# A decoder layer with dilated attention, short convolution and 32 experts: experts packed four to three blocks, and other orders around them

## The chip, the core and the metric

The kernel runs on one core of a Trainium2 chip. Its engines are TensorE (PE in the profile), VectorE (DVE), ScalarE (ACT), GpSimd (POOL) and SyncE (SP), which only issues transfers here. Each engine works through its own instructions in order and waits on semaphores; 16 DMA engines move data. The metric is the device time of one execution in microseconds, the median of several runs.

## The reference, cut to what matters

1024 prompt tokens and 32 sample tokens (8 sequences of 4) go through one layer. All is float32. The part around the change is this:

```python
h = h + mixed                                  # attention and convolution, one output projection
m = rms_norm(h, g_ffn)
g_sel = top_k(softmax(m @ w_router_group), 1)  # one of 4 groups
top_v, top_i = top_k((m @ w_router_expert)[group g_sel], 2)   # two of its 8 experts
hidden = silu(m @ w_gate[e]) * (m @ w_up[e]) * gates          # per chosen expert, 256 wide
h = h + sum over both experts of hidden @ w_down[e]
gate = sigmoid(rms_norm(h, g_ple) @ w_ple_gate)
h = h + (p @ w_ple_proj) * gate                # p: an embedding of 256 per token
```

Each of the 1056 tokens has two of 32 experts, so 2112 rows are worked on, 66 per expert in the mean. The router depends on the data.

## The kernel before

The order of work is written out by hand: each engine has its own program, and semaphores join them. Tokens come in nine tiles: eight prompt tiles of 128 rows, then one of 32 (the sample). There are seven parts: the input projection, the convolution, the attention over the prompt (32 steps, a pair of heads and a tile each, listed in `STEPS`), the attention of the sample over its cache, the output projection with the routing, the experts, and the last stage with the embeddings.

**Output projection and routing.** For tile t TensorE runs `out_att(t)`, `router(t-1)` (transposes of the normalised tile), `rank(t-2)`, `out_conv(t)`, `logits(t-1)`. VectorE adds the residual in two parts, `make_m` multiplies by the reciprocal root and the gain, `choose` finds the experts, and `place` works out where the token stands in its expert's list. `make_m` needs the sum of squares (ScalarE) and the root. GpSimd stores the tile m in DRAM (`store_m`) and writes the token numbers to the lists in DRAM (`enlist`), and after the last tile the lists of the first four experts are loaded. VectorE then orders the other 28 experts by their number of rows, largest first.

**Experts.** A block is 128 rows. `PLAN` says how the 28 ordered experts fall into blocks: F is one expert with up to 128 rows, P a pair with up to 64 rows each, in two column strips of TensorE's array. With the four first experts this makes 27 blocks; experts with more rows than their place holds get overflow blocks, which run only if there are any. Weights (3 MB an expert) go through four slots. A planner in Python gives each load its slot and the block after which the slot is free: SP loads gate and up weights when the up products of that block are done, and the down weights when its down products are done, in the order of the loads. In block n TensorE runs `up(n)`, `down(n-1)`, `trans_rows(n+1)` (transposes of the gathered rows, copied by VectorE in `take_rows`), `trans_hidden(n)`. GpSimd's program for the blocks is

```python
        for n in range(NBM):
            if n + NSTAT + 1 < NBM:
                fetch(n + NSTAT + 1)
            if n + 2 < NBM:
                pool.wait_ge(S("lists_in"), 16 * max(1, n + 4 - NSTAT))
                gather(n + 2, n % 2, lists[0:CAP, 2 * n + 4:2 * n + 5])
            scatter(n, n % 2, lists[0:CAP, 2 * n + 1:2 * n + 2])
```

`gather` loads rows of m from DRAM by a list (an indirect DMA), `scatter` waits for `rows_done` of block n (ScalarE has copied both halves of its down products) and stores them. So gather(n+2) is behind scatter(n-1) in this queue.

**Last stage.** For tile t: SP loads the two expert rows of each token (`load_h`) and the embedding rows, VectorE's `combine` adds them with their weights (h2) and, when ScalarE has the root of the mean square, multiplies by its reciprocal and the gain (hn). TensorE runs `embed(t)`, `gates(t)` (the product with the 1024 x 1024 gate matrix in two halves), `trans_p(t+1)`, `trans_h(t+1)`. ScalarE takes the sigmoid, and VectorE's `finish` multiplies it with the embedding product straight from PSUM and adds h2.

## Time and profile before

| what | before |
|---|---|
| median of 3 runs | 1403.39 us (1402.79 to 1406.4) |
| the profiled execution | 1402.83 us |
| its span, first to last instruction | 1401.0 us |
| TensorE, VectorE, ScalarE, GpSimd busy | 1215.4, 431.5, 326.2, 169.5 us |
| mean granted TensorE clock | 0.934 of full |
| moved by DMA | 209.15 MB |

The profile is of one execution. Busy time is the time in which an engine has an instruction in work; an idle stretch of an engine is put down to what released it. Rows of the trace give the start in us from the span's start and the duration. A product of float32 tiles appears as two MATMUL records. L-numbers are lines of the kernel before.

### The profile page before, as it was taken

Reading aid. Unit: us, or ns where it says so; the run is one execution under the profiler, and the core shown is the slowest. Engines: PE = TensorE matmul, PEld = TensorE weight load, DVE = VectorE, ACT = ScalarE, POOL = GpSimd, SP = SyncE. Lnnn points to the kernel's source line nnn. Section 1 sums busy time; section 2 is a strip of 40 time slices with the busy share of each in tenths; the row PEclk is TensorE's granted clock in tenths of the full one; section 3 lists DMA queues with packets and bytes.
Section 4 is the critical chain, followed back from the end, with each engine's and each line's share of the span. In section 5 each row is a group of like instructions: output and inputs, shape, how many; then the busy total and the mean of one; then the engine's idle time right before and its main releaser. Section 6 shows DMA issues by size and latency. Waiting matters only on the chain.

```text
span 1401.0 us, 13600 instructions
## 1 busy us (share of the span) xinstructions
PE 1215.4 (87%) x4994; PEld 651.9 (47%) x4994; DVE 431.5 (31%) x972; ACT 326.2 (23%) x637; POOL 169.5 (12%) x171
## 2 busy tenths in 40 slices
PE   4999999999978887866999938888889898789995
PEld 1444445666645555732455524444344434334442
DVE  1121212221147777311255581411111111033332
ACT  2132322000027664411011110111111111133332
POOL 0001000000030113000001131121212221000000
PEclk9999999999979998877999958999999999979998
DMA  8011400111050102879612054788888888522200
GB/s 271 36 45 60 124 15 19 45 41 64 0 159 31 31 2 62 236 217 325 247 61 72 37 199 140 274 302 354 299 340 300 340 306 344 223 93 98 92 29 34
DMA packets 63660, 209.15 MB, mean 149 GB/s; under 512 B 15198, under 2 KB 28926, under 8 KB 47728
## 3 DMA queue, kind: packets, MB, share of 16 engines
q1 hardware_dynamic: 50560, 177.64, 36.3%
q0 software_dynamic: 13040, 30.71, 5.7%
q8 instruction: 38, 0.62, 0.2%
q14 instruction: 22, 0.18, 0.0%
HBM read 191.81 MB, written 27.52 MB: 157 GB/s over the span
## 4 chain that ended last, share of the span: by engine, by line
PE 71%; DMA 12%; DVE 8%; issue 4%; ACT 3%; POOL 1%; SPq 1%; POOLq 0%; DVEq 0%; ACTq 0%
PE pair L1618 12%; PE pair L1670 12%; PE pair L1939 9%; PE pair L1855 8%; PE pair L2042 8%; DMA R<-m_dram,lists 7%; PE pair L1962 4%; DMA R<-in_cache_v 3%; PE pair L1697 3%; PE pair L1711 2%; PE pair L2024 2%; PE pair L1724 2%; DVE R L1455 2%; DVE R L1229 1%; PE pair L1748 1%
## 5 line engine op out<-in xcount | busy, mean ns | idle before, releaser
L1939 PE MATMUL pair<-R 128*128 128x512 f32 (+1 forms) x512 | 201.3, 617 | 19.9 <-DVE R L1455 19.9
L1670 PE MATMUL pair<-R 128*128 128x352 f32 x576 | 172.5, 463 | 0.4 <-ACT kts L868 0.4
L1618 PE MATMUL pair<-R 128*128 128x512 f32 x384 | 170.2, 601 | 0.8 <-DVE R L1121 0.8
L1670 PEld LDWEIGHTS pair<-R 128*128 128x128 f32 x576 | 110.2, 192 | 61.8 <-issue 1.5
L1939 PEld LDWEIGHTS pair<-R 128*128 128x128 f32 (+1 forms) x512 | 79.6, 180 | 124.8 <-issue 99.1
L1855 PE MATMUL pair<-R 128*128 128x512 f32 x256 | 115.5, 606 | 0.0
L2042 PE MATMUL pair<-R 128*128 128x512 f32 x256 | 114.2, 605 | 0.8 <-ACT R L1053 0.8
L1618 PEld LDWEIGHTS pair<-R 128*128 128x128 f32 x384 | 72.9, 193 | 87.5 <-issue 86.3
L1962 PE MATMUL pair<-R,bias_s 128*128 128x512 f32 (+1 forms) x256 | 98.0, 597 | 0.7 <-ACT bias_s L1009 0.7
L2042 PEld LDWEIGHTS pair<-R 128*128 128x128 f32 x256 | 49.7, 194 | 63.7 <-issue 63.7
L1460 DVE TENSOR_TENSOR R<-pair,R 128x256 f32<-128x256 f32 x27 | 11.5, 425 | 206.6 <-ACT R L1005 206.5
L1855 PEld LDWEIGHTS pair<-R 128*128 128x128 f32 x256 | 48.4, 194 | 55.9 <-issue 55.9
L1455 DVE COPY R<-pair 128x512 f32<-128x512 f32 x54 | 35.0, 686 | 100.3 <-PE pair L1925 100.1
L1711 PE MATMUL pair<-ident,R 128*128 128x128 f32 x288 | 45.0, 296 | 23.0 <-DVE R L1229 17.1
L1962 PEld LDWEIGHTS pair<-R,bias_s 128*128 128x128 f32 (+1 forms) x256 | 38.3, 173 | 56.5 <-issue 55.6
L1005 ACT ACTIVATE R<-pair 128x256 f32<-128x256 f32 x27 | 10.3, 383 | 223.7 <-PE pair L1939 223.7
L765 POOL DMA_INDIRECT y_dram<-R,lists x27 | 27.1, 1005 | 283.9 <-ACT R L1017 263.3
L1925 PE MATMUL pair<-ident,R 128*128 128x128 f32 x216 | 31.9, 293 | 28.7 <-DMA R<-m_dram,lists 28.6
L917 ACT ACTIVATE R<-pair 128x512 f32<-128x512 f32 (+3 forms) x96 | 43.6, 484 | 42.6 <-PE pair L1711 42.3
L1711 PEld LDWEIGHTS pair<-ident,R 128*128 128x128 f32 x288 | 32.9, 148 | 41.4 <-DVE R L1229 36.9
L906 ACT ACTIVATE R<-R,small 128x1024 f32<-128x1024 f32 (+7 forms) x64 | 49.4, 772 | 6.7 <-DVE small L1220 6.2
L1220 DVE CUSTOM_DVE_ANT_0 R<-pair,R 128x1024 f32<-128x1024 f32 (+7 forms) x64 | 45.8, 753 | 14.0 <-PE pair L1697 13.8
(280 smaller groups left out, 1280.9 us busy)
## 6 DMA issues: line engine op xcount, KB each, us to landing
R<-in_w_gate SPq DMA_DIRECT2D x32, 1024.0 KB, 8.3
R<-in_w_up SPq DMA_DIRECT2D x32, 1024.0 KB, 11.1
R<-in_w_down SPq DMA_DIRECT2D x32, 1024.0 KB, 5.0
R<-in_x_prompt SPq DMA_DIRECT2D x16, 512.0 KB, 3.4
R<-in_cache_k SPq DMA_DIRECT2D x8, 1024.0 KB, 9.1
R<-in_cache_v SPq DMA_DIRECT2D x8, 1024.0 KB, 18.6
R<-y_dram SPq DMA_DIRECT2D x16, 512.0 KB, 4.3
R<-in_w_in SPq DMA_DIRECT2D x3, 2048.0 KB, 14.9
```

The lines of the kernel that those rows point to most:

```text
L906: act.activation(E[n % 2][hh][:, 0:w], E[n % 2][hh][:, 0:w], ACT.Exp, bias=nmax[:, k:k + 1], scale=-1.0, accum_out=den[:, k:k + 1]).then_i ...
L917: act.activation(PTb[n % 2][hh][:, j0:j0 + m, :], bk[4 + use % 2].rearrange("p (a b) -> p a b", b=P)[:, 0:m, ::-1], ACT.Copy).then_inc(S(" ...
L1220: dve.tensor_tensor_reduce(E[n % 2][hh][:, 0:w], bank[hh][:, 0:w], Z[2 * (pair % 2) + hh][:, SEQ - w:SEQ], -1.0, 3e38, ALU.add, ALU.min, n ...
L1455: dve.tensor_copy(xgT[u][:, 4 * j:4 * j + 4, :], bk[j][:, 0:4 * CAP].rearrange("p (g n) -> p g n", g=4)).then_inc(S("rowsT_done"), 1)
L1618: last = mm(bk[4 + part][0:n, :], xTs[a.u][:, c, 0:n], wA[:, c, AD * part:AD * part + AD], start=(c == 0), stop=(c == DC - 1))
L1670: last = mm(bk[b][:, 0:n], wB[q % 2][:, c, which, :], xT[:, c, lo:lo + n], start=(c == 0), stop=(c == DC - 1))
L1697: last = mm(bank[hh][:, c0:c0 + m], QT[half, pair, P * i:P * i + P], KT[half, pair, c0:c0 + m], start=True, stop=True)
L1711: last = pe.transpose(bk[4 + use % 2][:, P * j:P * j + P], E[n % 2][hh][:, P * (j0 + j):P * (j0 + j) + P], ident[:, :])
L1855: last = mm(bk[2 * pair + j][0:n, :], lhs[:, q, P * a.t:P * a.t + P], w_out[:, c0 + q, 512 * j:512 * j + 512], start=(q == 0), stop=(q == ...
L1939: last = mm(bk[2 + u][r, :].rearrange("p (w f) -> p w f", w=2), xgT[u][:, c, r], wgu[s][:, :, c, :], start=(c == 0), stop=(c == DC - 1))
L1962: last = mm(bk[4 + j][r, :], hT[u][:, q, r], wd[s][:, q, 512 * j:512 * j + 512], start=(q == 0), stop=(q == 1))
L2042: last = mm(bk[2 + j][0:n, :], hnT[a.u][:, c, 0:n], w_pg[c][:, 512 * j:512 * j + 512], start=(c == 0), stop=(c == DC - 1))
```

## The change

- **Blocks.** `PLAN` gets a third kind, T: four experts make three blocks. Three of them have a block each, with up to 96 rows in three column strips of 32, and the fourth gives 32 of its rows to the fourth strip of each. With 4 F, 3 T and 6 P there are 23 blocks. The fourth expert's weights are loaded first and stay for three blocks. `up` and `down` go by parts (first column, width, slot). The limit of overflow blocks goes from 24 to 32.
- **Order within a block.** `trans_rows(n+1)` stands ahead of `down(n-1)` instead of behind it.
- **Routing.** The router's transposes take h times the gain (`gain_m`), without the root; the logits are multiplied by the reciprocal root when they leave PSUM, and the stored tile is multiplied by it in place (`scale_m`) after the transposes. The sample's tile comes second instead of last (`turned`). The running counts start with the list bases; `rank` has three products (counts, first choice, second choice) in place of two, and `place` and `choose` lose one small operation each. The load of the first four lists is issued by SP instead of GpSimd, ahead of the fourth expert's weights.
- **Last stage.** All nine tiles' embedding products are made before the loop, ScalarE copies them to SBUF, and the embeddings are loaded in two transfers. In the loop TensorE runs `gates(t, 0)`, `trans_h(t+1)`, `gates(t, 1)`. The transposes take h2 times the gain, and the reciprocal root (`rms_f`) goes into the sigmoid's scale. `load_h(t)` waits for the finished output of tile t-2, where it waited for its h2.
- **Attention.** The tiles of a pair of heads go from 7 down to 0.

The core of the diff:

```diff
 
-STEPS = [(pair, i) for pair in range(NG) for i in (7, 0, 6, 1, 5, 2, 4, 3)]
+STEPS = [(pair, i) for pair in range(NG) for i in (7, 6, 5, 4, 3, 2, 1, 0)]
...
 NSTAT = 4
-PLAN = "FFPFFFFPFFFPFFFFPFFFPFF"
+PLAN = "PFTPFTPFTPFPP"
+NFULL = NSTAT + PLAN.count("F")
+NTRI = PLAN.count("T")
+NPAIR = PLAN.count("P")
+FULL = ((0, 128, 0),)
+PAIR = ((0, 64, 0), (64, 64, 1))
+TRI = ((0, 32, 0), (32, 32, 0), (64, 32, 0), (96, 32, 1))
...
     for kind in PLAN:
+        l = len(ranks)
         if kind == "F":
-            blocks.append(((len(loads),), NSTAT + f))
-            loads.append(("rank", f))
-            f += 1
+            ranks.append(full)
+            blocks.append(Blk((l,), FULL, NSTAT + full))
+            full += 1
+        elif kind == "T":
+            first = NFULL - NSTAT + 4 * tri
+            ranks += [first + 3, first, first + 1, first + 2]
+            for j in range(3):
+                blocks.append(Blk((l + 1 + j, l), TRI, NFULL + 3 * tri + j))
+            tri += 1
         else:
-            blocks.append(((len(loads), len(loads) + 1), NSTAT + nfull + p))
-            loads.append(("rank", nfull + 2 * p))
-            loads.append(("rank", nfull + 2 * p + 1))
-            p += 1
+            first = NFULL - NSTAT + 4 * NTRI + 2 * pair
+            ranks += [first, first + 1]
+            blocks.append(Blk((l, l + 1), PAIR, NFULL + 3 * NTRI + pair))
+            pair += 1
     last = {}
-    for n, (members, _) in enumerate(blocks):
-        for l in members:
+    for n, b in enumerate(blocks):
+        for l in b.loads:
...
+
+def turned(i):
+
+    t = 0 if i == 0 else PT if i == 1 else i - 1
+    return Tile(t, i % 2, i // 2, P if t < PT else SAMP, i)
...
         load_down(2, LSLOT[2])
+        sp.wait_ge(S("list_out"), 16 * 2 * TILES)
+        sp.dma_start(lists[:, 0:2 * NSTAT].rearrange("p (e c) -> p e c", c=2),
+                     list_dram.rearrange("(e r) c -> r e c", r=LROWS)[0:CAP, 0:NSTAT, :]).then_inc(S("static_in"), 16)
...
             if not a.early:
-                sp.wait_ge(S("h2_done"), a.t - 1)
-                sp.wait_ge(S("pT_full"), a.t - 1)
+                sp.wait_ge(S("out_done"), a.t - 1)
             lo = y_dram[SEQ:TOK, :] if a.rows == SAMP else y_dram[bass.ds(a.t * P, P), :]
             hi = y_dram[TOK + SEQ:2 * TOK, :] if a.rows == SAMP else y_dram[TOK:2 * TOK, :][bass.ds(a.t * P, P), :]
...
-        def make_m(a):
+        def gain_m(i):
+            a = turned(i)
             n, u = a.rows, a.u
-            dve.wait_ge(S("mean"), a.t + T + 1)
+            dve.wait_ge(S("h_done"), pieces(i + 1))
+            if i >= 2:
+                dve.wait_ge(S(f"out{u}"), 16 * (a.k + USES[u]))
+            dve.tensor_tensor(m_st[u][0:n, :], h[0:n, a.t, :], gffn[0:n, :], ALU.mult).then_inc(S("hg_done"), 1)
+
+        def scale_m(i):
+            a = turned(i)
+            n, u = a.rows, a.u
+            dve.wait_ge(S("mean"), i + T + 1)
             dve.reciprocal(rsh[0:n, u:u + 1], msh[0:n, u:u + 1]).then_inc(S("rstd"), 1)
-            dve.wait_ge(S("rstd"), a.t + T + 1)
-            if not a.early:
-                dve.wait_ge(S("xT_full"), 2 * (a.t + T) - 2)
-                dve.wait_ge(S(f"out{u}"), 16 * (a.k + USES[u]))
-            dve.scalar_tensor_tensor(m_st[u][0:n, :], h[0:n, a.t, :], rsh[0:n, u:u + 1], gffn[0:n, :],
-                                     ALU.mult, ALU.mult).then_inc(S("m_done"), 1)
+            dve.wait_ge(S("rstd"), i + T + 1)
+            dve.wait_ge(S("hg_done"), i + 1)
...
-            dve.wait_ge(S("lg_full"), t + 1)
-            dve.tensor_copy(lg[0:n, t, :], bk[7][0:n, 0:RG]).then_inc(S("logits_done"), 1)
+            dve.wait_ge(S("lg_full"), i + 1)
+            dve.tensor_scalar(lg[0:n, t, :], bk[7][0:n, 0:RG], rsh[0:n, u:u + 1], None, ALU.mult).then_inc(S("logits_done"), 1)
+            dve.wait_ge(S("logits_done"), i + 1)
...
+        def rank(i):
+            a = turned(i)
+            n, u = a.rows, a.u
+            pe.wait_ge(S("chosen"), i + 1)
+            if i >= 1:
+                pe.wait_ge(S("pos_done"), i)
+                pe.wait_ge(S("cum_done"), i)
+            mm(bk[4][0:n, 0:NE], ones[:, 0:n], r_cum[1 - u], start=True, stop=False)
+            for k in range(2):
+                last = mm(bk[4][0:n, 0:NE], tri[0:n, 0:n], r_h[u][k][0:n, :], start=False, stop=(k == 1))
             last.then_inc(S("rank_full"), 1)
...
         def members(n):
-            return [(LSLOT[l], LCOUNT[l]) for l in BLOCKS[n][0]]
+            b = BLOCKS[n]
+            return [(lo, m, LSLOT[b.loads[k]], LCOUNT[b.loads[k]]) for lo, m, k in b.parts]
 
         trans_rows(0, 0, 16)
         for n in range(NBM):
             up(n, n % 2, members(n))
+            if n + 1 < NBM:
+                trans_rows(n + 1, (n + 1) % 2, 16 * uses_of(n + 1))
             if n >= 1:
                 down(n - 1, (n - 1) % 2, members(n - 1))
-            if n + 1 < NBM:
-                trans_rows(n + 1, (n + 1) % 2, 16 * uses_of(n + 1))
             trans_hidden(n, n % 2)
...
+            dve.wait_ge(S("h2_done"), a.t + 1)
+            if not a.early:
+                dve.wait_ge(S("xT_full"), 2 * (a.t + 2 * T) - 2)
+            dve.tensor_tensor(hn[u][0:n, :], h2[u][0:n, :], gple[0:n, :], ALU.mult).then_inc(S("hn_done"), 1)
+
+        def rms_f(a):
+            n, u = a.rows, a.u
             dve.wait_ge(S("ms"), a.t + T + 1)
-            dve.reciprocal(rsf[0:n, u:u + 1], msf[0:n, u:u + 1]).then_inc(S("rstd"), 1)
-            dve.wait_ge(S("rstd"), a.t + 2 * T + 1)
-            dve.scalar_tensor_tensor(hn[u][0:n, :], h2[u][0:n, :], rsf[0:n, u:u + 1], gple[0:n, :],
-                                     ALU.mult, ALU.mult).then_inc(S("hn_done"), 1)
...
         combine(fixed(0))
-        over_tiles(dve, step_h)
+        for t in range(TILES):
+            if t + 1 < TILES:
+                combine(fixed(t + 1))
+            rms_f(fixed(t))
+            finish(t)
...
+        def gate(t, j):
+            a = fixed(t)
             n = a.rows
+            if j == 0:
+                act.wait_ge(S("rsf_done"), t + 1)
+                if t >= 2:
...
+            act.wait_ge(S("gate_full"), 2 * t + j + 1)
+            act.activation(gs[a.u][0:n, 512 * j:512 * j + 512], bk[2 + j][0:n, :], ACT.Sigmoid,
+                           scale=rsf[0:n, a.u:a.u + 1]).then_inc(S("gate_done"), 1)
...
         pe.wait_ge(S("rows_done"), 2 * NBM)
-        trans_p(fixed(0))
+        pe.wait_ge(S("p_in"), 32)
+        turn_p(0)
+        turn_p(1)
         pe.wait_ge(S("wpp_in"), 32)
-        embed(fixed(0))
-        trans_h(fixed(0))
+        for t in range(TILES):
+            embed(t)
+            if t + 2 < TILES:
+                turn_p(t + 2)
+            if t == PT - 1:
+                trans_h(0)
         pe.wait_ge(S("wpg_in"), 16 * DC)
-        over_tiles(pe, step_h)
+        pe.wait_ge(S("pp_done"), 2 * PT + 4)
+        for t in range(PT):
+            gates(t, 0)
+            trans_h(t + 1)
+            gates(t, 1)
+        gates(PT, 0)
 
```

## Rows read from the trace of the kernel before

**Rows 1.** The page, busy time, share and instructions of TensorE.
```profile
PE 1215.4 (87%) x4994; PEld 651.9 (47%) x4994; DVE 431.5 (31%) x972; ACT 326.2 (23%) x637; POOL 169.5 (12%) x171
```

**Rows 2.** Windows: length; busy PE, PEld, DVE, ACT, POOL; clock, DMA share, GB/s.
```profile
402.00:547.00 145.00, 119.10 (x1004) 78.52 (x1006) 103.38 (x284) 91.60 (x221) 29.93 (x12) 0.91 0.13 39
669.30:800.80 131.50, 131.50 (x432) 68.94 (x432) 61.08 (x188) 18.00 (x36) 13.96 (x17) 0.98 0.30 110
800.80:846.10 45.30, 17.86 (x152) 14.02 (x150) 32.57 (x104) 7.42 (x14) 16.07 (x17) 0.60 0.44 168
846.10:1214.90 368.80, 331.62 (x1030) 151.22 (x1030) 58.33 (x117) 52.22 (x107) 72.62 (x72) 0.97 0.78 298
1214.90:1234.40 19.50, 6.14 (x20) 3.38 (x19) 6.50 (x6) 5.06 (x9) 0.97 (x1) 0.71 0.55 201
1234.40:1386.70 152.30, 151.92 (x472) 72.94 (x472) 50.38 (x54) 49.52 (x79) 4.35 (x8) 0.98 0.19 69
```

**Rows 3.** Timeline of PE, blocks 0 to 3: start us, us, line, operation [idle <-releaser].
```profile
843.36 1.94 PE L1925 MATMUL pair<-ident,R 128*128 128x128 f32 x8 [13.21 <-DMA R<-m_dram,lists]
...
868.29 1.06 PE L1925 MATMUL pair<-ident,R 128*128 128x128 f32 x8
...
870.34 7.13 PE L1939 MATMUL pair<-R 128*128 128x512 f32 x16 [0.76 <-DVE R L1455]
...
877.31 3.60 PE L1962 MATMUL pair<-R,bias_s 128*128 128x512 f32 x8
...
881.56 1.15 PE L1925 MATMUL pair<-ident,R 128*128 128x128 f32 x8 [0.65 <-DMA R<-m_dram,lists]
```

**Rows 4.** Timeline of POOL: gather 0, scatter 0, gather 3.
```profile
839.08 1.05 POOL L757 DMA_INDIRECT R<-m_dram,lists  x1 [2.56 <-DMA lists<-list_dram]
...
870.05 1.03 POOL L765 DMA_INDIRECT y_dram<-R,lists  x1 [22.91 <-ACT R L1017]
...
872.72 1.00 POOL L757 DMA_INDIRECT R<-m_dram,lists  x1 [0.31 <-issue]
```

**Rows 5.** DMA issues of the whole span: KB each, median us to landing.
```profile
R<-y_dram SPq DMA_DIRECT2D x16, 512.0 KB, 4.3
...
R<-m_dram,lists POOLq DMA_INDIRECT x27, 9.4
```

**Rows 6.** Groups of PE by form: busy us, mean ns, idle before.
```profile
L1939 PE MATMUL pair<-R 128*128 128x512 f32 x352 | 165.9, 627 | 16.1 <-DVE R L1455 16.1
...
L1939 PE MATMUL pair<-R 128*64 128x512 f32 x160 | 35.4, 595 | 3.8 <-DVE R L1455 3.8
...
L1925 PE MATMUL pair<-ident,R 128*128 128x128 f32 x216 | 31.9, 293 | 28.7 <-DMA R<-m_dram,lists 28.6
...
L1761 PE MATMUL pair<-R 128*32 128x512 f32 x64 | 7.3, 594 | 1.4 <-ACT R L940 1.4
```

**Rows 7.** Timeline behind two released slots: the gather, and TensorE behind it.
```profile
1023.87 1.00 POOL L757 DMA_INDIRECT R<-m_dram,lists  x1 [0.31 <-issue]
...
1035.54 1.97 PE L1925 MATMUL pair<-ident,R 128*128 128x128 f32 x8 [3.05 <-DMA R<-m_dram,lists]
...
1038.29 9.14 PE L1939 MATMUL pair<-R 128*128 128x512 f32 x16 [0.36 <-DVE R L1455]
```

**Rows 8.** Timeline of the last stage, tile 0 and the start of tile 1.
```profile
1234.38 16.93 PE L2042 MATMUL pair<-R 128*128 128x512 f32 x32 [0.78 <-ACT R L1053]
...
1252.36 3.69 PE L2024 MATMUL pair<-R 128*128 128x512 f32 x8
...
1252.78 1.22 DVE L1561 TENSOR_TENSOR R<-R 128x1024 f32<-128x1024 f32 x1
...
1254.21 1.28 DVE L1533 SCALAR_TENSOR_TENSOR R<-R,w 128x1024 f32<-128x1024 f32 x1 [0.21 <-DVE R L1561]
...
1255.89 13.90 PE L2042 MATMUL pair<-R 128*128 128x512 f32 x32
```

**Rows 9.** Timeline of PE in the tail: the sample's router transposes.
```profile
817.44 1.08 PE L1871 MATMUL pair<-ident,R 32*128 32x32 f32 x8 [2.26 <-DVE R L1355]
```

More of the change, by code:

```diff
@@ L358, in _build @@
     r_ms, r_cand, r_rb, r_prod = (tk(NE) for _ in range(4))
-    r_a, r_cum = ([tk(NE) for _ in range(2)] for _ in range(2))
+    r_cum = [tk(NE) for _ in range(2)]
     r_pen = tk(GROUPS)
@@ L640, in load_h @@
             sp.dma_start(y1[a.u][0:a.rows, :], hi).then_inc(S(f"in{a.u}"), 16)
-            if not a.first:
-                load_p(a)
         load_h(fixed(0))
@@ L728, in _ @@
         pool.wait_ge(S("code_in"), 16)
-        for t in range(TILES):
-            store_m(fixed(t))
-            if t >= 2:
-                enlist(t - 2)
+        for i in range(TILES):
+            if i >= 2:
+                enlist(i - 2)
+            store_m(i)
         enlist(TILES - 2)
@@ L1063, in gate @@
                 return
-            for j in range(2):
-                act.wait_ge(S("gate_full"), 2 * a.t + j + 1)
-                if j == 0 and not a.early:
-                    act.wait_ge(S("out_done"), a.t - 1)
-                act.activation(gs[a.u][0:n, 512 * j:512 * j + 512], bk[2 + j][0:n, :], ACT.Sigmoid).then_inc(S("gate_done"), 1)
-        def step_h(prev, cur, nxt):
-            if nxt is not None:
-                square_f(nxt)
-            gate(cur)
-            if nxt is not None:
-                evac_pT(nxt)
-                evac_hnT(nxt)
@@ L1396, in choose @@
-            dve.wait_ge(S("cum_done"), t + 1)
-        def place(a):
+            dve.tensor_scalar(h2_, desc[0:n, :], cm, None, ALU.is_equal).then_inc(S("chosen"), 1)
+            dve.wait_ge(S("chosen"), i + 1)
+            if n == SAMP:
+                then(dve.tensor_copy(r_cum[u], r_cum[1 - u]))
+                then(dve.tensor_tensor(r_cum[u][0:n, :], r_cum[u][0:n, :], h1, ALU.add))
+            else:
+                then(dve.tensor_tensor(r_cum[u], r_cum[1 - u], h1, ALU.add))
+            dve.tensor_tensor(r_cum[u][0:n, :], r_cum[u][0:n, :], h2_, ALU.add).then_inc(S("cum_done"), 1)
@@ L1420, in _ @@
-        place(fixed(TILES - 2))
-        choose(fixed(TILES - 1))
-        place(fixed(TILES - 1))
+        for i in range(TILES):
+            residual_att(i)
+            if i >= 1:
+                scale_m(i - 1)
+            if i >= 2:
+                place(i - 2)
+            residual_conv(i)
+            gain_m(i)
+            if i >= 1:
+                choose(i - 1)
+        scale_m(TILES - 1)
+        place(TILES - 2)
+        choose(TILES - 1)
+        place(TILES - 1)
         dve.wait_ge(S("cnt_full"), 1)
-        dve.tensor_copy(r_cc, bk[0][:, 0:NE]).then_inc(S("cnt_done"), 1)
+        dve.tensor_tensor(r_cc, bk[0][:, 0:NE], base, ALU.subtract).then_inc(S("cnt_done"), 1)
@@ L1545, in finish @@
+            if not a.early:
[3 more added lines that the diff above has]
+            n, u = a.rows, a.u
+            dve.wait_ge(S("ms"), a.t + T + 1)
+            dve.reciprocal(rsf[0:n, u:u + 1], msf[0:n, u:u + 1]).then_inc(S("rsf_done"), 1)
+        def finish(t):
+            a = fixed(t)
             n, u = a.rows, a.u
-            if not a.early:
+            if t >= 2:
@@ L1849, in out_part @@
             for j in range(2):
-                if not a.first:
-                    pe.wait_ge(S(done), 2 * a.t + j - 1)
+                if i >= 1:
+                    pe.wait_ge(S(done), pieces(i) if i == 2 else pieces(i) - 1 + j)
                 for q in range(CC):
-                    if a.first and j == 0:
+                    if i == 0 and j == 0:
                         pe.wait_ge(S(f"wout_in{(c0 + q) // 2}"), 32)
@@ L1899, in _ @@
         pe.wait_ge(S("ssc"), 5)
-        for t in range(TILES):
-            out_att(fixed(t))
-            if t >= 1:
-                router(fixed(t - 1))
-            if t >= 2:
-                rank(fixed(t - 2))
-            out_conv(fixed(t))
-            if t >= 1:
-                logits(fixed(t - 1))
-        router(fixed(TILES - 1))
-        rank(fixed(TILES - 2))
-        logits(fixed(TILES - 1))
-        rank(fixed(TILES - 1))
+        for i in range(TILES):
+            out_att(i)
+            if i >= 1:
+                router(i - 1)
+            if i >= 2:
+                rank(i - 2)
+            out_conv(i)
+            if i >= 1:
+                logits(i - 1)
+        router(TILES - 1)
+        rank(TILES - 2)
+        logits(TILES - 1)
+        rank(TILES - 1)
         pe.wait_ge(S("cum_done"), TILES)
```

378 lines of the change are left out of this document (195 added, 183 removed).

## The prediction

> **What bounds the kernel now.** I read the page first: TensorE is busy 87% of the span [rows 1], so the first question for every edit is whether it takes TensorE work away or puts a wait into it. Then the stretches [rows 2]. In this order they are attention over the prompt, output projection, tail of the routing (from the end of the last prompt tile's projection to the first expert product), 27 expert blocks, a gap, and the last stage (gate products). The reader is to see three kinds. In the projection and in the last stage TensorE is busy all the time (131.50 of 131.50, 151.92 of 152.30 us). In the routing tail and the gap it mostly waits (17.86 of 45.30, 6.14 of 19.50). The expert stage is between them, 331.62 of 368.80, 13.7 us for each of 27 blocks, with the DMA engines at 0.78.
>
> What a block waits for is in the order of time [rows 3, 4]. TensorE ends block 0's down products at 868.3, GpSimd issues the scatter of that block's rows at 870.05, then a fetch of a list, and at 872.72 the gather of the rows of block 3. TensorE turns these rows at 881.56, after 0.65 us of idle. So from the end of down products to the gather's issue it is 4.4 us, and from issue to use 8.84; over all 27 gathers the median landing takes 9.4 [rows 5]. In the old order up(2) and down(1) lie between down(0) and the turning of block 3, so that this chain of 13.3 us is hidden behind 12.6 us of work and shows as 0.65 us.
>
> **Four experts to three blocks.** 27 blocks become 23. A pair block's 160 product records of 64 columns are busy 35.4 us for 5 blocks, 7.1 a block; the 352 of full blocks 165.9 us for 22 blocks, 7.5 [rows 6]. So two strips run beside each other. Four strips of 32 columns in the sample's scores: 64 records of 128x512 are busy 7.3 us, 8 steps of four strips at 0.91 us, where a full block takes 0.9 us a step. A block of the new kind should therefore cost what a full one does, and four blocks fewer are worth at most 4 x 13.7 = 55 us. The weights are read as before (28 chosen experts, 3 MB each). By the planner seven blocks instead of four now free two weight slots at once. Rows for the gather are no fewer in all. The new limits hold for the reference's inputs: of the 28 experts the fifth by number of rows has 85 (limit 96), the seventeenth 57 (limit 64), so no overflow block runs.
>
> **The order within a block.** This is the part that decides. The new order is up(n), turn rows(n+1), down(n-1), turn hidden(n). It hides VectorE's copies, 0.76 us of idle before each up [rows 3]. But GpSimd's program is as it was: gather(n+1) stands behind scatter(n-2), which waits for down(n-2). In the new order only turn hidden and up, 7.5 us, lie between down(n-2) and the turning of rows n+1, and down(n-1) is queued behind that turning. So one block now has to last as long as the whole chain: 4.4 (down to gather issue) + landing + 1.0 (turning) + 3.5 (down) us. Before, two blocks shared one such chain. For the landing: without other traffic it is at most 4.3 (issued 839.08, used 843.36) [rows 3, 4]; single bursts of weights give 8.84; a double burst gives 11.67 (1023.87 to 1035.54) [rows 7]. The burst is released by the same end of down products as before, so the contention stays. With 9.4 for 13 blocks and 11.2 for 7 I take 10.0: a block of 18.9 us. Down(0) ends at about 868.6 as before. 20 such blocks, less 4 us because the last three have no fetch, bring the end of down(20) to 1242.6, and up(22), down(21) and down(22) with their turns add 16: 1258.7 against 1214.9, **+44 us**. The bounds of the landing, 8.8 and 11.7, make this +20 and +78.
>
> **The clock in these waits.** TensorE now idles 5.7 us or more in every block. After an idle of 3.05 us (turning and little else around it) the eight transposes took 1.97 instead of 1.06 us and the up products 9.14 instead of 7.13 [rows 3, 7], which is the 1.2 GHz level for a while. Transposes and down products lie on the chain, so this costs between 0 and 0.9 + 2.0 = 2.9 us a block. I take 1.6, since only some waits of the old stage show it, and those of the new one are longer: **+32 us**. The Trainium skill (TensorE: Matmul & The Clock Gate, section "HAM oscillation — how this bites in real kernels") says that a kernel which waits for a DMA in every tile restarts every tile at the low clock. The trace shows it after some waits only. By that rule the loss would be whole each time; that case stands below, priced from rows.
>
> **The last stage.** The 18.5 us period is 13.90 of gates, 1.06 of transposes and 3.69 of embedding products [rows 8], all TensorE. The embedding products go ahead of it, into the gap in which the expert rows are fetched. There they cost 8 x 3.69 + 1.1 = 31 us, some 2 us of transposes, about 4 us until the two larger loads of embeddings and weights have landed (one MB each, behind a 512 KB transfer's 4.3 [rows 5]), and 1.6 us to turn tile 0 and copy the last products. The gap grows from 19.5 to about 38, **+18.5**. The loop should fall from 18.5 to 15 us a tile. But the load of the expert rows now waits for out_done of two tiles before, where it waited for the finished sum h2. The chain: end of gates to the end of the output's addition 2.7 us (1234.38 + 16.93 to 1252.78 + 1.22), issue of two loads and landing 0.2 + 0.5 + 4.3, two multiply-adds and one product 1.28 + 1.28 + 1.22, transposes 1.06, second half of the gates 6.95; with 0.4 for gaps, 19.9 us [rows 5, 8]. TensorE wants the rows after the first half, at 6.95, and gets them at about 12. So a tile takes 20 us in seven of eight steps: 15 + 7 x 20 - 3 (the sample's small tile) + 3.9 = 156 against 152.3, **+3.7**. Together +22. Idle of 5 us a step lowers the clock again, 0 to 2.9 each, the bound from [rows 7]; I take 1.8: **+13**. If the loads were early, the stage would gain 14 in all (+18.5, less 8 x 3.69 and the 3.0 that the first gates lost, 16.93 for 13.90).
>
> **Routing on un-normalised tiles, the sample second.** Before, the tail holds two passes through the router, and the second, the sample's, begins with its transposes at 817.44, 28.7 us before the first expert product [rows 2, 9]. With the sample second the last pass begins at about 803.3, since the transposes need only one product of VectorE (1.22) and neither the square, the root nor the reciprocal. With 1.5 us for the larger tile the tail is 33 us for 45.3. Into the busy part go 6 us of sample products and 1.5 us for a third rank product in each of nine tiles: **-5 us**, bounds -9 and 0. The scaling of the stored tile is hidden in VectorE's idle half (61.08 of 131.50 busy [rows 2]); without that cover it would be 1.2 us a tile. The list's load moves from GpSimd's queue to SP's behind one expert's loads, which were issued long before; nothing.
>
> **Attention order** (7..0 for 7,0,6,1,...): the same instructions, no engine full (TensorE 119, VectorE 103 of 145 us [rows 2]). Long tiles follow each other without short ones between, and short ones come together at the end. I take 0, bounds -4 and +5.
>
> **Sum:** 0 - 5 + 44 + 32 + 22 + 13 = +106 against the profiled execution's 1402.83 us (span 1401.0), which lies 0.6 under the median of 1403.39: **1509 us**.
>
> **The rivals.** (a) Both waits appear, but the clock stays at its high level: 1403 - 5 + 44 + 22 = **1464**. For it: the old stage waited 28.6 us for gathers (13.2 of them ahead of the first block) and kept a mean clock of 0.97 [rows 2, 3, 6]. (b) Each restart is cold in full: 20 x 2.9 + 7 x 2.9 = 78 in place of 45, **1542**. For it: the idle is twice that of [rows 7]; against it: the products after the wait may raise the clock sooner. (c) Faster: the gathers land early, since fewer bytes move in each us. At 4.5 us a block is 13.4, down(20) ends at 1133, the stage at 1149: -66 - 5 + 22 = -49, **1354**. The whole is even where the landing is 7.0 us (a block of 15.9); the gather beside a single burst took 8.84, over the median's 27 it is 9.4, and only the unburdened one took 4.3, and the burst is released at the same moment. (d) The strips do not overlap, and the nine new blocks cost three more times their 11 us, about **1800**; [rows 6] speak against it.
>
> **How the numbers follow.** A difference under 0.3% (4 us) can't be told from none here. Forecast 0.50, (a) 0.20, (b) 0.18, (c) 0.07, (d) 0.01; 0.04 remains for one wait alone, partly near zero. Faster 0.07, same 0.02, slower 0.91. The range from 1450 to 1558 takes in (a) and (b) and the landing's bounds.
>
> **What would show it.** In the changed kernel's profile: about 5 to 6 us of idle before nearly every turning of rows, released by the gather, where it was 28.6 us in all; blocks of 18 to 21 us; GpSimd's gather 4.4 us after down products; idle before the last stage's transposes, released by VectorE's product, behind a load issued right after the output's addition; a granted clock well below 0.97 in the expert stage. I am wrong if the turning of rows starts within a us of the up products, or if four-strip blocks take over 9 us for up.

## The result, and the profile after

The changed kernel takes 1545.16 us (median of 4 runs, 1533.87 to 1554.48) against 1403.97 for the kernel before in the same session: ratio 1.100, 95% interval 1.0915 to 1.1085. It is slower by 141 us, 36 us above the forecast of 1509 and inside its range. The profiled execution has a span of 1537.9 us, 136.9 more than before.

The page of the changed kernel: busy time, and in 40 slices the granted clock. TensorE is as busy as before in us [rows 1], so what was added is idle time; the products that are gone with four blocks are made up for by products at a lower clock, in the expert blocks and the last stage, where the clock's row shows its run of eights.
```profile
PE 1218.9 (79%) x5550; PEld 637.0 (41%) x5550; DVE 432.2 (28%) x966; ACT 328.3 (21%) x643; POOL 157.2 (10%) x158
...
PEclk9999999999799987789995888887888888998888
```
Windows of the changed kernel, columns as in [rows 2]: output projection, tail of the routing, expert blocks, gap (with the embedding products in it), gate products.
```profile
665.60:805.50 139.90, 139.66 (x541) 74.16 (x540) 74.27 (x226) 20.00 (x41) 18.39 (x22) 0.99 0.28 105
805.50:844.20 38.70, 11.77 (x64) 10.82 (x62) 23.47 (x71) 5.43 (x9) 11.71 (x11) 0.55 0.50 193
844.20:1301.50 457.30, 323.96 (x1566) 130.85 (x1566) 55.69 (x106) 42.10 (x91) 60.52 (x60) 0.83 0.62 237
1301.50:1346.80 45.30, 33.67 (x109) 16.43 (x107) 7.50 (x6) 15.29 (x33) 0.97 (x1) 0.89 0.31 113
1346.80:1522.70 175.90, 136.15 (x384) 65.36 (x384) 48.13 (x54) 53.02 (x77) 4.37 (x8) 0.89 0.19 59
```
Against [rows 2] the first expert product starts 1.9 us earlier, the blocks take 88.5 us more, the gap 25.8, the gates' stage 23.6, and what follows it 0.9: -1.9 + 88.5 + 25.8 + 23.6 + 0.9 = 136.9. In the blocks the clock fell from 0.97 to 0.83 and the DMA share from 0.78 to 0.62: neither engine nor transfers are full.

Where TensorE waited, in the view of waits (total, times, longest). L2006 is the turning of rows, that is the transposes of a block's gathered rows, which had waited 28.6 us in all before [rows 6]; L2087 is the transposes of the last stage and L2076 those of the embeddings.
```profile
PE pair L2006 <- DMA R<-m_dram,lists: 150.2, 21, 18.2
PE pair L2087 <- DVE R L1614: 38.9, 7, 6.8
...
PE pair L2076 <- DMA R<-in_p_sample: 9.8, 1, 9.8
```
One block on TensorE and on GpSimd (columns as in [rows 3] and [rows 4]).
```profile
880.60 1.97 PE L2006 MATMUL pair<-ident,R 128*128 128x128 f32 x8 [5.58 <-DMA R<-m_dram,lists]
882.37 4.63 PE L2041 MATMUL pair<-R,bias_s 128*128 128x512 f32 x8
886.84 0.39 PE L2028 MATMUL pair<-ident,R 128*128 128x128 f32 x2
887.06 7.03 PE L2019 MATMUL pair<-R 128*128 128x512 f32 x16
900.29 1.97 PE L2006 MATMUL pair<-ident,R 128*128 128x128 f32 x8 [6.20 <-DMA R<-m_dram,lists]
```
```profile
888.57 1.01 POOL L798 DMA_INDIRECT y_dram<-R,lists  x1 [15.39 <-ACT R L1051]
889.88 1.03 POOL L781 DMA_INDIRECT lists<-list_dram,idx_i  x1 [0.30 <-issue]
891.21 1.00 POOL L790 DMA_INDIRECT R<-m_dram,lists  x1 [0.30 <-issue]
```
The reader sees the ring that the forecast described: down products, scatter, gather, turning, and the next down products behind it. Rows are turned at 880.60, down products end at 887.00, the scatter is issued at 888.57, the gather at 891.21, its rows are turned at 900.29. That is 1.8 + 4.6 + 4.2 + 9.1 = 19.7 us for one block, and the up products of 7.03 us lie inside it without filling it. Over 19 such blocks (880.60 to 1279.67) the mean is 21.0.

### The profile page after: what moved, and what is told of

The parts are those of the page before. It is cut to its first block, busy times and chain, and to the rows that moved or that the text cites. A ratio compares the mean times of both kernels' runs of the same rounds, so it can differ in the third digit from the quotient of the medians.

```text
span 1537.9 us, 14460 instructions
## 1 busy us (share of the span) xinstructions
PE 1218.9 (79%) x5550; PEld 637.0 (41%) x5550; DVE 432.2 (28%) x966; ACT 328.3 (21%) x643; POOL 157.2 (10%) x158
## 3 DMA queue, kind: packets, MB, share of 16 engines
q1 hardware_dynamic: 50976, 177.64, 33.3%
## 4 chain that ended last, share of the span: by engine, by line
PE 61%; DMA 21%; DVE 7%; issue 4%; ACT 3%; POOL 2%; SPq 1%; POOLq 0%; ACTq 0%; DVEq 0%
DMA R<-m_dram,lists 13%; PE pair L1695 11%; PE pair L1747 11%; PE pair L1933 7%; PE pair L2041 7%; PE pair L2126 5%; DMA R<-in_cache_v 3%; PE pair L2006 3%; DMA R<-y_dram 2%; PE pair L1774 2%; PE pair L1788 2%; PE pair L2107 2%; PE pair L2019 2%; PE pair L1801 2%; POOL lists L781 1%
## 5 line engine op out<-in xcount | busy, mean ns | idle before, releaser
L1695 PE MATMUL pair<-R 128*128 128x512 f32 x384 | 169.9, 600 | 0.8 <-DVE R L1176 0.8
L2019 PE MATMUL pair<-R 128*32 128x512 f32 (+2 forms) x896 | 165.7, 598 | 1.5 <-DVE R L1527 1.5
L2006 PE MATMUL pair<-ident,R 128*128 128x128 f32 x184 | 43.5, 413 | 150.2 <-DMA R<-m_dram,lists 150.2
L2126 PE MATMUL pair<-R 128*128 128x512 f32 x256 | 120.2, 630 | 1.7 <-ACT R L1091 1.7
L1933 PE MATMUL pair<-R 128*128 128x512 f32 x256 | 115.5, 605 | 0.0
L2041 PE MATMUL pair<-R,bias_s 128*32 128x512 f32 (+2 forms) x448 | 113.4, 784 | 0.5 <-ACT bias_s L1043 0.5
L2006 PEld LDWEIGHTS pair<-ident,R 128*128 128x128 f32 x184 | 35.1, 217 | 168.8 <-DMA R<-m_dram,lists 149.6
L2019 PEld LDWEIGHTS pair<-R 128*32 128x32 f32 (+2 forms) x896 | 55.9, 128 | 94.3 <-issue 90.4
L1527 DVE COPY R<-pair 128x512 f32<-128x512 f32 x46 | 31.6, 690 | 144.8 <-PE pair L2006 142.9
L1049 ACT ACTIVATE R<-pair 128x512 f32<-128x512 f32 x23 | 13.7, 597 | 233.9 <-PE pair L2041 233.9
L798 POOL DMA_INDIRECT y_dram<-R,lists x23 | 23.1, 1005 | 387.0 <-ACT R L1051 370.0
L2041 PEld LDWEIGHTS pair<-R,bias_s 128*32 128x32 f32 (+2 forms) x448 | 34.3, 167 | 66.3 <-issue 65.6
L1788 PE MATMUL pair<-ident,R 128*128 128x128 f32 x288 | 45.2, 289 | 14.2 <-DVE R L1284 8.5
L1774 PE MATMUL pair<-R 64*128 64x512 f32 (+3 forms) x192 | 44.2, 568 | 7.9 <-DVE small L1275 7.4
```

Source lines behind the costliest of these rows:

```text
L1527: dve.tensor_copy(xgT[u][:, 4 * j:4 * j + 4, :], bk[j][:, 0:4 * CAP].rearrange("p (g n) -> p g n", g=4)).then_inc(S("rowsT_done"), 1)
L1695: last = mm(bk[4 + part][0:n, :], xTs[a.u][:, c, 0:n], wA[:, c, AD * part:AD * part + AD], start=(c == 0), stop=(c == DC - 1))
L1774: last = mm(bank[hh][:, c0:c0 + m], QT[half, pair, P * i:P * i + P], KT[half, pair, c0:c0 + m], start=True, stop=True)
L1788: last = pe.transpose(bk[4 + use % 2][:, P * j:P * j + P], E[n % 2][hh][:, P * (j0 + j):P * (j0 + j) + P], ident[:, :])
L1933: last = mm(bk[2 * pair + j][0:n, :], lhs[:, q, P * a.t:P * a.t + P], w_out[:, c0 + q, 512 * j:512 * j + 512], start=(q == 0), stop=(q == ...
L2006: last = pe.transpose(bk[j][:, CAP * (c % 4):CAP * (c % 4) + CAP], xg[u][:, c:D:DC], ident[0:CAP, 0:CAP])
```

## The experiments

All stage times below are read from the timelines of the profiled executions: blocks from the first up product to the last down product, gap to the first gate product, gates to the last one. Each ratio is to the kernel before as run in the same session, where its median was 1398.7 to 1404.0 us; the differences in us below are between medians.

| kernel | median us | ratio to before (95%) | blocks | gap | gates |
|---|---|---|---|---|---|
| before | 1403.97 | | 368.8 | 19.5 | 152.3 |
| changed | 1545.16 | 1.100 (1.0915 to 1.1085) | 457.3 | 45.3 | 175.9 |
| 1 changed, old order | 1418.51 | 1.010 (1.0036 to 1.0169) | 339.7 | 42.8 | 180.0 |
| 2 before, new order | 1559.16 | 1.110 (1.1024 to 1.1176) | 527.2 | 19.4 | 151.7 |
| 3 changed, rows at h2 | 1481.68 | 1.055 (1.0473 to 1.0618) | 454.3 | 44.7 | 122.9 |
| 4 both of 1 and 3 | 1362.14 | 0.971 (0.9634 to 0.9786) | 340.2 | 45.1 | 122.9 |
| 5 changed, gather ahead | 1411.61 | 1.006 (1.0022 to 1.0089) | 327.0 | 45.2 | 179.4 |
| 6 changed, small loads | 1390.51 | 0.992 (0.9891 to 0.9948) | 305.5 | 44.0 | 176.5 |
| 7 changed, filler | 1505.72 | 1.074 (1.0694 to 1.0782) | 425.6 | 45.3 | 174.0 |
| 8 both of 5 and 3 | 1354.57 | 0.965 (0.962 to 0.9674) | 326.9 | 45.7 | 122.9 |
| 9 as 8, 27 blocks | 1350.71 | 0.962 (0.9571 to 0.9661) | 322.3 | 42.7 | 122.9 |
| 10 before, attention order | 1395.19 | 0.995 (0.9928 to 0.9972) | 372.0 | 19.4 | 152.3 |
| 11 as 8, gate weights later | 1352.03 | 0.964 (0.96 to 0.9672) | 325.9 | 42.9 | 122.9 |
| 12 before, 2 and gather ahead | 1352.67 | 0.967 (0.9632 to 0.9705) | 320.3 | 19.5 | 151.2 |

**1. Old order in the changed kernel.**
```diff
             up(n, n % 2, members(n))
-            if n + 1 < NBM:
-                trans_rows(n + 1, (n + 1) % 2, 16 * uses_of(n + 1))
             if n >= 1:
                 down(n - 1, (n - 1) % 2, members(n - 1))
+            if n + 1 < NBM:
+                trans_rows(n + 1, (n + 1) % 2, 16 * uses_of(n + 1))
             trans_hidden(n, n % 2)
```


> The changed kernel with one thing put back: down products of block n-1 stand ahead of the turning of rows n+1 again. Theory A (the order within the block made the gather's chain last one block): the waits of the turning of rows, 150.2 us in the changed kernel, fall to under 30; a block takes 13.7 us as before, 23 of them 315 us in place of 457.3, up to 330 if the double bursts of weights make some gathers late; the whole 1545 - 127 to - 142, about 1410. Rival B (the bursts of the new plan, or four experts in one block, keep the gathers late whatever the order): a block stays above 17 us and the whole above 1480. Rival C (24 experts of 3 MB in 315 us is more than the DMA engines give, which were 0.78 busy over 368.8 us): the waits move to the weights, the stage ends at 345 or more.


The blocks fell by 117.6 us and the wait of the turnings to 33.3 in all. Theory A holds for the cause, 8 us over its time: the stage is 339.7, not 315 to 330, and waits on the up weights have appeared. That is a little of rival C.
```profile
PE pair L2006 <- DMA R<-m_dram,lists: 33.3, 12, 18.2
PE pair L2019 <- DMA R<-in_w_up: 16.2, 4, 5.5
```

**2. New order in the kernel before** (the reverse of that edit).


> The kernel before with one thing changed: the turning of rows n+1 stands ahead of down products of block n-1. 27 blocks, old plan of loads. Theory A (order alone): 23 or 24 blocks of 19.5 to 21 us in place of 13.7, so +135 to +175, the whole 1540 to 1580, with 5 us or more of wait before nearly each turning. Rival B (the order costs that much only with the new plan's double bursts): blocks under 16.5 us and the whole under 1470.


1559.2: theory A. The order alone costs 155 us, more than the whole change, so the double bursts aren't needed for it. After the start every turning waited 5.4 to 8.5 us and took 1.97 us.
```profile
PE pair L1925 <- DMA R<-m_dram,lists: 159.8, 25, 13.3
```

**3. The last stage's load back at h2.**
```diff
             if not a.early:
-                sp.wait_ge(S("out_done"), a.t - 1)
+                sp.wait_ge(S("h2_done"), a.t - 1)
```


> The changed kernel with one thing put back: in the last stage the load of the expert rows of tile t+2 waits for the finished sum h2 of tile t, not for out_done. Theory A (that wait holds TensorE): the transposes' wait on VectorE's product, 38.9 us in the changed kernel, falls to under 8, seven steps take 15 to 16 us in place of 22 to 23, so -45 to -52, the whole about 1495. Rival B (the sum of tile t+1 stands behind the output of tile t-1 on VectorE anyway, which holds it as long): steps stay above 20 us, the whole within 15 us of 1545.


Theory A. In the trace of this kernel the transposes follow the gates without a wait, and both are at their short durations, at a granted clock of 1.00 over this stage (0.89 in the changed kernel):
```profile
1366.03 1.16 PE L2087 MATMUL pair<-ident,R 128*128 128x128 f32 x8
1367.03 13.90 PE L2126 MATMUL pair<-R 128*128 128x512 f32 x32
1380.79 1.16 PE L2087 MATMUL pair<-ident,R 128*128 128x128 f32 x8
1381.79 13.90 PE L2126 MATMUL pair<-R 128*128 128x512 f32 x32
```
In the changed kernel the same rows are
```profile
1375.28 1.97 PE L2087 MATMUL pair<-ident,R 128*128 128x128 f32 x8 [6.78 <-DVE R L1614]
1377.04 15.06 PE L2126 MATMUL pair<-R 128*128 128x512 f32 x32
1397.81 1.97 PE L2087 MATMUL pair<-ident,R 128*128 128x128 f32 x8 [5.71 <-DVE R L1614]
```
with the output's addition on VectorE ahead of the load on SyncE's queue:
```profile
1386.72 1.22 DVE L1639 TENSOR_TENSOR R<-R 128x1024 f32<-128x1024 f32 x1
1388.13 0.33 SPq L676 DMA_DIRECT2D R<-y_dram  x1
```
A tile takes 14.76 us in place of some 22.5, the stage 53.0 less. The median fell by 63.5, the profiled spans by 55.4; the rest is scatter between runs.

**4. Both put back.**


> The changed kernel with both put back: old order in the block, load of the expert rows at h2. If the two waits and the clock that they cost are all of the loss, the gains add: 1545 - 135 - 49 = about 1361, which is 42 us under the kernel before (four blocks fewer -50, last stage -2, start and tail of the routing -2, gap). If a third cause holds time (four-strip blocks, the load of the weights, the longer gap), it stays above 1390.


1362.1. Alone the two edits are worth 126.7 and 63.5 us and together 183.0, so the two causes are nearly independent. Together they are more than the whole loss of 141: without them the change is 42 us faster than the kernel before.

**5. The gather ahead of the scatter.**
```diff
         fetch(NSTAT)
+        gather(2, 0, lists[0:CAP, 4:5])
         for n in range(NBM):
             ...
-            if n + 2 < NBM:
-                if n + 2 >= NSTAT:
-                    pool.wait_ge(S("lists_in"), 16 * (n + 3 - NSTAT))
-                gather(n + 2, n % 2, lists[0:CAP, 2 * n + 4:2 * n + 5])
+            if n + 3 < NBM:
+                if n + 3 >= NSTAT:
+                    pool.wait_ge(S("lists_in"), 16 * (n + 4 - NSTAT))
+                gather(n + 3, (n + 1) % 2, lists[0:CAP, 2 * n + 6:2 * n + 7])
             scatter(n, n % 2, lists[0:CAP, 2 * n + 1:2 * n + 2])
```


> The changed kernel, new order in the block kept; on GpSimd the gather of block n+3 now stands ahead of the scatter of block n (before: behind it), so it no longer waits for down products of block n, only for the turning of rows n+1, and two blocks lie between its issue and its use. Theory A (the loss is not the order by itself but the gather queued behind the scatter that waits for down): the gathers are hidden as in the first experiment, its wait of 33 us or less, and the time is that of the first experiment, 1418, or up to 12 us below it, since the order now hides VectorE's copies (0.76 us a block). Rival B (a gather issued earlier collides with more weights and lands later, or the fetches and scatters behind it hold the next): waits above 80 us, the whole above 1460.


Theory A, in the form it was put. TensorE's new order is harmless once the gather no longer stands behind a scatter that waits for down: no turning waits any more but the first. Against the first experiment the stage is 12.7 us shorter, but the intervals of the two ratios overlap. The waits have moved to the weights:
```profile
PE pair L2088 <- DVE R L1615: 40.1, 7, 7.0
PE pair L2020 <- DMA R<-in_w_up: 37.9, 8, 10.5
...
PE pair L2007 <- DMA R<-m_dram,lists: 18.1, 1, 18.1
```

**6. Small loads.** Of each expert's weights from the fifth on, only the first eighth is read (the first 256 of 2048 columns of gate, up and down weights), so its output is computed with partly old weights.
```diff
-            load_wide(e, LSLOT[l])
+            s = LSLOT[l]
+            sp.dma_start(SLOTS[s][:, 0:256], wg_r[e][:, 0:256]).then_inc(S(f"w_in{s}"), 16)
+            sp.dma_start(SLOTS[s][:, 2048:2304], wu_r[e][:, 0:256]).then_inc(S(f"w_in{s}"), 16)
...
-            load_down(e, LSLOT[l])
+            sp.dma_start(SLOTS[s][:, 4096:4352], wd_r[e][:, 0:256]).then_inc(S(f"wd_in{s}"), 16)
```


> The changed kernel with its order, but the weights of the chosen experts from the fifth on are loaded in their first eighth only (768 of 6144 columns), each at its old place in the queue; the rest of a slot keeps the columns of an earlier expert. Theory A (the gather lands late because it shares the DMA engines with the weights): it lands in 4.3 to 5.5 us in place of about 9, a block takes 13.5 to 15 us in place of 21, and the clock's loss goes with most of the wait: 1545 - 120 to - 150, about 1410. Rival B (the chain is GpSimd's issues and the clock, not the traffic): a block still takes over 17.5 us, the whole stays above 1470.


Theory A, 5 us below its range. The issues of the whole span, first of this kernel, then of the changed one:
```profile
R<-m_dram,lists POOLq DMA_INDIRECT x23, 4.2
```
```profile
R<-m_dram,lists POOLq DMA_INDIRECT x23, 9.4
```
The same gather lands in 4.2 us when the weights are small. A block takes 13.4 us (the mean of 19), with turnings of 1.15 us behind waits of 0.8 to 2.4. That is rival (c) of the prediction, 13.4 us a block for a landing of 4.5, and here it took the removal of seven eighths of these weights' traffic.

**7. Filler.**
```diff
+            if 3 <= n < NBM - 1:
+                for _ in range(5):
+                    mm(bk[6], ident[:, :], xgT[n % 2][:, 0:4, :], start=True, stop=True)
             if n + 1 < NBM:
                 trans_rows(n + 1, (n + 1) % 2, 16 * uses_of(n + 1))
...
             gates(t, 0)
+            for _ in range(5):
+                mm(bk[6], ident[:, :], w_pg[0][:, 0:512], start=True, stop=True)
             trans_h(t + 1)
```


> The changed kernel with work added in TensorE's waits: five products of 128x512 (about 0.88 us each at the high clock, 4.4 us in all, into a bank that nobody reads) ahead of each turning of rows from block 4 on, and five ahead of each tile's transposes in the last stage. Nothing else reads or waits for them. Theory A (the turning's 1.97 us in place of 1.06, the down products' 4.5 to 5.8 in place of 3.6 and the gates' 14.5 to 16 in place of 13.9 are the low clock after idle): the added work makes the kernel faster, by 0.9 + 1.6 for each of 20 blocks and 0.9 + 1.3 for each of 7 tiles, so -45 to -65, the whole 1480 to 1500, with the turning back at 1.1 to 1.2 us. Rival B (they are slow for another reason, such as contention with the loads): no gain, 1540 to 1560. Rival C (the filler is longer than the shortened wait): the wait is gone and the blocks stay near 20 us.


121.7 us of useless products made the kernel 39 us faster. Theory A in kind, somewhat under its size (39 for 45 to 65). Groups of TensorE by form in the filled kernel (busy, mean ns, idle before), and under them those of the changed kernel:
```profile
L2053 PE MATMUL pair<-R,ident 128*128 128x512 f32 x190 | 86.1, 600 | 0.0
...
L2041 PE MATMUL pair<-R,bias_s 128*32 128x512 f32 x288 | 35.4, 636 | 0.0
...
L2006 PE MATMUL pair<-ident,R 128*128 128x128 f32 x184 | 31.2, 322 | 64.2 <-DMA R<-m_dram,lists 64.2
```
```profile
L2041 PE MATMUL pair<-R,bias_s 128*32 128x512 f32 x288 | 46.3, 800 | 0.0
L2006 PE MATMUL pair<-ident,R 128*128 128x128 f32 x184 | 43.5, 413 | 150.2 <-DMA R<-m_dram,lists 150.2
```
The turning fell from 413 to 322 ns a product; the down products of the nine four-strip blocks fell from 46.3 to 35.4 us. Of rival C one half came: blocks with the filler still lasted 19.3 us in the mean, against 21.0, but the wait wasn't gone; 64.2 us of it stayed, 18.3 of them ahead of the first block. After 0.9 to 1.8 us of remaining wait the transposes took 1.15 to 1.17 us. After 2.5 to 4.3 us they were mostly slow, but not always (1.79 after 2.56, 1.57 after 3.83, 1.97 after 3.29, but 1.15 after 2.50 and after 3.65).

**8. Gather ahead and rows at h2.**


> The changed kernel with the gather ahead of the scatter (as in the fifth experiment) and the load of the expert rows at h2 (as in the third). If the fifth finds its wait gone, the two gains add as those of the first and the third did (127 and 63.5 alone, 183 together): 1545 - 127 - 60 - 0 to 12, so 1350 to 1362; if the early gather collides with the weights it stays above 1400.


1354.6, as expected.

**9. The same with the plan of 27 blocks** (PLAN as before, the lines for four strips left out).


> The eighth experiment's kernel (1354.6 us: new order, gather ahead of scatter, rows loaded at h2) with the plan of the kernel before: 27 blocks, full and pairs, no four-strip blocks. It isolates what four experts in three blocks are worth. Theory A (TensorE sets the stage): four blocks of 12.6 to 13.4 us more, so +50 to +54, the whole 1405 to 1409. Rival B (with 23 blocks the weights' loads are already the bound, as 36 us of waits on them in the eighth experiment speak for): of the 52 us only what those waits leave, 52 - 30 = 22 or less, the whole 1367 to 1380.


Both forecasts of the time were wrong: it isn't slower at all. The windows of the expert blocks, of the ninth kernel and then of the eighth:
```profile
843.10:1165.40 322.30, 316.85 (x1030) 149.03 (x1030) 58.34 (x117) 49.63 (x107) 73.52 (x73) 0.98 0.87 341
```
```profile
846.70:1173.60 326.90, 286.19 (x1566) 115.34 (x1566) 51.84 (x106) 42.23 (x91) 61.47 (x61) 0.93 0.86 333
```
With 27 blocks TensorE is busy 316.85 of 322.3 us and waits 0.5 us for up weights: its own products set the stage, as theory A has it. Four experts in three blocks took 30.7 us of products off it, and in the eighth kernel it waited instead, as rival B has it:
```profile
PE pair L2020 <- DMA R<-in_w_up: 36.0, 8, 10.2
```
The DMA engines move nearly the same bytes in both, at 0.86 to 0.87 busy. What limits the loads in the eighth isn't separated: SyncE stood 243.7 us waiting for down products to free a slot, so it can be the rate of the transfers or the moment at which they may start. The two intervals overlap, so with hidden gathers this part of the change is worth nothing that was measured.

**10. The attention order alone.**


> The kernel before with one thing changed: the order of the attention steps, 7 to 0 in place of 7, 0, 6, 1, 5, 2, 4, 3. The prediction put 0 on it, with bounds -4 and +5; in the changed kernel the output projection starts 3.8 us earlier than in the kernel before. Theory A: that is this order, so 1400, -3 to -4. Rival B: it comes from elsewhere or is the scatter between executions (the same stretch starts at different times in the experiments): within 2 us of the kernel before.


6.3 us faster, 4 to 10 by the interval: theory A in kind, above its size, and rival B is out. In the one profiled execution the output projection starts 6.7 us earlier than in the kernel before, which fits a gain in the attention, though starts in single traces differ by some us.

**11. Gate weights behind the embeddings** (the eight loads moved to after the loads of the embeddings).


> The eighth experiment's kernel with one order changed on SyncE's queue: the eight loads of the gate weights (4 MB, wanted only after all embedding products) are issued behind the loads of embeddings and embedding weights instead of ahead of them. Theory A (these 4 MB hold up the embeddings, on which TensorE waits 8.6 us in the gap): they land in 7 to 8 us in place of 11.7, the wait falls to 3 to 5, so -4 to -5, the whole about 1350. Rival B (they then land too late for the gates or hold up the expert rows): no gain or a loss of up to 5.


The wait fell from 8.6 to 6.3 us and the gap by 2.8; the time by 2.5, inside both intervals. Kernels with the loads in their old order waited 5.8 (9) to 9.8 us (the changed one), so this doesn't show what the embeddings wait for.

**12. Two moves in the kernel before** (the edits of 2 and of 5).


> The kernel before with two moves only: the turning of rows n+1 ahead of down products of block n-1 (the second experiment's edit, which alone cost 155 us), and on GpSimd the gather of block n+3 ahead of the scatter of block n. Everything else, 27 blocks, attention order, routing, last stage, is as before. Theory A (the new order is good as soon as its gather doesn't wait for down): blocks of 11.6 us as in the ninth experiment in place of 13.7, the stage about 322 in place of 368.8, so -43 to -47, the whole 1355 to 1360; with the ninth experiment at 1350.7 all other parts of the change together are then worth under 10 us. Rival B (the gain of the ninth experiment is from the other parts): 1385 to 1405.


1352.7, theory A. The same order that cost 155 us alone gains 46 together with the gather one place earlier. Which of the two moves gains how much isn't shown, since no run has the gather ahead in the old order. In the stage the waits for gathers fell from 15.4 us to none and those for VectorE's copies from 19.9 to 2.2, and the first of these may not need the new order. The ninth kernel has these two moves and the rest of the change but for the new blocks, and takes 1350.7: the two intervals overlap, so nothing is measured for all that rest together, though the attention order alone gave 6.3. A block is turning, down products, the turning of the hidden rows and up products, without a wait between them:
```profile
908.37 1.05 PE L1926 MATMUL pair<-ident,R 128*128 128x128 f32 x8
909.25 3.60 PE L1963 MATMUL pair<-R,bias_s 128*128 128x512 f32 x8
912.69 0.39 PE L1949 MATMUL pair<-ident,R 128*128 128x128 f32 x2
913.01 7.09 PE L1940 MATMUL pair<-R 128*64 128x512 f32 x32
920.02 1.15 PE L1926 MATMUL pair<-ident,R 128*128 128x128 f32 x8
```

## Why the prediction was right, and where its sizes were off

The mechanism, the sign and the range were right; the likeliest case was 31 us short against the span (+106 for +136.9). Term by term, with the span's times:

**Order within a block: +44 forecast, 41 measured.** Of the 88.5 us, about 48 are slower products (next point); the other 41 are the balance of longer waits and of the work of four blocks, which is gone. The landing was taken at 10.0 us; from the gather's issue to the turning it was 8.3 to 11.9 in the 20 blocks that waited, 9.9 in the mean, so this term was right in its parts too. The experiments show each link: the scatter in the gather's way (5), the weights in its landing (6), the order as the trigger (1, 2).

**The clock in these waits: +32 forecast, 48 measured. This is the term that was mis-sized.** It was set at 1.6 us a block, between 0 and 2.9, because the old stage showed slow products after some waits only. After waits of 5.2 us and more the turning took 1.97 or 1.98 us every time, 20 of 20 (1.94 ahead of the first block). The 23 turnings took 43.5 us in place of 23 x 1.1, so 18; the 448 records of down products 113.4 us in place of 23 x 3.62, so 30. The up products were at their short duration again, 7.03 to 7.09 us. So in kind it was rival (b), every restart cold, while the price of 2.9 a block, of which 2.0 were read from up products, was too high: with turning and down products it was about 2.4. The seventh experiment shows that idle causes it, and the third agrees for the last stage, where both durations are short once the wait is gone. That the median came within 3 us of rival (b)'s 1542 is luck: with the last stage the clock cost 62 us, midway between the forecast's 45 and the rival's 78, and a longer wait in the last stage made up the difference. The Trainium skill (TensorE: Matmul & The Clock Gate, section "HAM oscillation — how this bites in real kernels") says that a loop which waits for a DMA in each round starts each round at the low clock. All 20 turnings agree with it, at 1.97 or 1.98 us for 1.06.

**Last stage, the wait: +22 forecast, 35 measured.** The gap grew by 25.8 instead of 18.5: the embeddings were waited for 9.75 us behind the last down products (forecast 4). Why so long stays open: 4 MB of gate weights are issued ahead of them, which the forecast had not counted, but moving these (11) changed no more than differs between kernels anyway. The products themselves took the 31 us forecast. In the gates' stage the waits were 38.9 us, 7 times, where 7 x 5 were forecast: +9.5 for +3.7.

**Last stage, the clock: +13 forecast, 14 measured.** Transposes 13.9 + 120.2 us of gates, against 8 x 1.1 and 8 x 13.9. With the 38.9 us of wait that makes the 53.0 by which the third experiment's stage is shorter.

**Routing and the sample second: -5 forecast, +2 measured.** The busy part is 139.9 for 131.5 us (+8.4, forecast +7.5), the tail 38.7 for 45.3 (-6.6, forecast -12.3). **Attention order: 0 forecast, -3.7 in this trace, -6.3 alone (10)**, a little outside the bound of -4. The start of the expert blocks lies between 838.8 and 846.7 in the ten kernels that are alike up to there (the changed one, 1, 3 to 9 and 11), so these few us aren't to be read from single traces. No experiment took the routing alone.

**Four experts to three blocks.** That four strips cost what a full block does is right: 63.7 us for nine blocks' up products is 7.08 each, and rival (d) is out. But what the edit is worth, "at most 55 us", depends on what sets the stage. Between 27 and 23 blocks lie 69.9 us where the ring of the gather sets the block (experiment 2 and the changed kernel), about 30 in the old order (before and experiment 1), and -4.6 with hidden gathers, where 27 blocks are set by TensorE's products and 23 wait for the weights (9 and 8). The forecast looked for the harm of the planner's double bursts in the gathers. With the old order or the gather ahead the waits stood on the up weights instead (16.2 us in 1, 37.9 in 5); that the double bursts make them isn't shown.

The embedding products ahead of the last stage, with the wait mended, take 45.7 + 122.9 us (8) for 19.5 + 152.3: 3 us less, where the forecast gave 14 for that case. Of the missing 11, 7.7 are the longer gap (45.7 for 38).

## What to carry to other kernels

When an instruction is moved up in one engine's order, look at what its input's transfer is queued behind on the issuing engine: here the new order lost 155 us with the gather behind one scatter, which waited for the work just moved back, and with the gather ahead of it the two moves gained 46. This stage had two resources near full, products and weights, and a saving of 31 us on one of them brought nothing, so work out both bounds before counting blocks. A wait in every round of a loop costs its own length and then the slow restart, which was 62 of the 137 us here.

## What was not expected of the hardware

Useless products in a wait can pay: 121.7 us of them saved 39. The indirect gathers of 128 rows landed in 4.2 us (median) in the kernel whose expert stage moved 105 GB/s and in 9.4 in the one whose stage moved 237. And the slow restart needs more than a short wait: in experiment 7, after 0.9 to 1.8 us, the eight transposes took 1.15 us, in the changed kernel, after 5.2 and more, always 1.97, and in between both occur (1.15 after 3.35 in experiment 4, 1.97 after 3.29 in experiment 7).
